# Products of w_out between the first scores of a delta rule, and the rule's level masks and spread rows on other engines

## What is computed

```
x += 0.5 * post1(FFN_a(pre1(x)))
h  = pre2(x);  u = h @ w_in          # columns for four mixers: pooling, RWKV-7, convolution, attention
x += post2(concat(A, B, C, D) @ w_out)
x += 0.5 * post3(FFN_b(pre3(x)))
```

```
s_kk = S @ kk
S    = S * w - outer(s_kk, kk * a) + outer(v, k)
y    = S @ r
```

## Time and profile before

| | |
|---|---|
| runs | 2569.2, 2569.83, 2566.56 us |
| the profiled execution's own time | 2568.88 us |
| its span, first to last instruction | 2567.1 us |
| mean granted clock of TensorE | 0.993 |
| PE busy | 2505.6 us, 98% |
| DVE busy | 1535.0 us, 60% |
| POOL busy | 1000.2 us, 39% |
| ACT busy | 945.5 us, 37% |

### The profile page before, as it was taken

One profiled execution on the slowest core, in us unless ns is written; L12 is line 12 of the kernel. 1 busy time (PEld: TensorE's weight loads), 2 busy tenths in 40 slices (PEclk: granted clock), 3 DMA queues, 4 the chain that ended last, 5 costly groups with the idle time before them and its releaser, 6 DMA issues.

```text
span 2567.1 us, 49724 instructions
## 1 busy us (share of the span) xinstructions
PE 2505.6 (98%) x20230; PEld 2444.3 (95%) x20230; DVE 1535.0 (60%) x2361; ACT 945.5 (37%) x1500; POOL 1000.2 (39%) x584
## 2 busy tenths in 40 slices
PE   8999999999899999999999999999998999999998
PEld 8999999999789999999999999998987889999998
DVE  6767721866774767771277767038567657777603
ACT  5444511422522444441244444133144244444412
POOL 4454532532112544543344544334312044545431
PEclk9999999999999999999999999999999999999999
DMA  4232222323102232222222232222230022222221
GB/s 118 85 88 82 82 72 61 97 58 94 45 3 76 58 91 82 82 85 73 74 66 82 82 90 76 76 79 70 68 98 17 11 67 83 82 82 82 83 77 64
DMA packets 356072, 188.64 MB, mean 73 GB/s; under 512 B 16330, under 2 KB 354086, under 8 KB 355912
## 3 DMA queue, kind: packets, MB, share of 16 engines
q1 hardware_dynamic: 355668, 186.25, 25.1%
q10 hardware_dynamic: 244, 0.08, 0.0%
HBM read 179.50 MB, written 6.80 MB: 73 GB/s over the span
## 4 chain that ended last, share of the span: by engine, by line
PE 88%; DVE 6%; DVEq 2%; ACT 2%; issue 1%; ACTq 0%; DMA 0%; SPq 0%
PE ps L1848 14%; PE ps L1850 13%; PE ps L1849 13%; PE ps L1971 12%; PE ps L1970 12%; PE ps L1969 12%; PE ps L1894 3%; PE ps L1837 1%; DVE xT L1197 1%; DVE ps L1193 1%; PE ps L2396 1%; PE ps L2414 1%; DVE h_split L1217 1%; PE ps L2410 1%; PE ps L2084 1%
## 5 line engine op out<-in xcount | busy, mean ns | idle before, releaser
L643 POOL TENSOR_TENSOR w_lo<-w_raw,w_hi 128x1024 fp32r<-128x1024 f32 (+1 forms) x186 | 444.9, 2396 | 949.6 <-ACT w_hi L724 948.6
L1848 PE MATMUL ps<-h_split,w_hi 128*128 128x384 f32 (+1 forms) x1536 | 485.0, 316 | 2.7 <-DVEq L1304 2.7
L1850 PE MATMUL ps<-h_split,w_lo 128*128 128x384 f32 (+1 forms) x1536 | 476.9, 310 | 0.0
L1849 PE MATMUL ps<-hidden_lo,w_hi 128*128 128x384 f32 (+1 forms) x1408 | 433.1, 308 | 0.0
L724 ACT ACTIVATE w_hi<-w_raw 128x1024 fp32r<-128x1024 f32 (+1 forms) x186 | 188.9, 1020 | 507.8 <-DMA w_raw<-in_ffn_w_down 318.3
L1849 PE MATMUL ps<-h_split,w_hi 128*128 128x256 f32 (+1 forms) x1152 | 354.8, 308 | 0.0
L1848 PEld LDWEIGHTS ps<-h_split,w_hi 128*128 128x128 f32 x1536 | 288.6, 188 | 8.6 <-issue 7.7
L1850 PEld LDWEIGHTS ps<-h_split,w_lo 128*128 128x128 f32 x1536 | 291.1, 190 | 0.0
L662 POOL TENSOR_TENSOR w_lo<-w_raw,w_hi 128x512 fp32r<-128x512 f32 x144 | 186.2, 1293 | 254.9 <-DVEq L1332 254.9
L1970 PE MATMUL ps<-h_split,w_hi 128*128 128x320 f32 x864 | 266.4, 308 | 0.0
L1971 PE MATMUL ps<-h_split,w_lo 128*128 128x320 f32 x864 | 266.4, 308 | 0.0
(11 more groups left out here) (390 smaller groups left out, 5808.8 us busy)
## 6 DMA issues: line engine op xcount, KB each, us to landing
w_raw<-in_ffn_w_gate SPq DMA_DIRECT2D x88, 512.0 KB, 4.6
w_raw<-in_ffn_w_up SPq DMA_DIRECT2D x88, 512.0 KB, 3.8
w_raw<-in_ffn_w_down SPq DMA_DIRECT2D x64, 448.0 KB, 3.4
w_raw<-in_w_in SPq DMA_DIRECT2D x42, 512.0 KB, 4.1
w_raw<-in_ffn_w_down SPq DMA_DIRECT2D x32, 512.0 KB, 3.7
w_raw<-in_w_out SPq DMA_DIRECT2D x16, 512.0 KB, 3.8
token_rows<-in_x_prompt SPq DMA_DIRECT2D x4, 512.0 KB, 5.9
k_cache<-in_cache_sb_k SPq DMA_DIRECT2D x2, 1024.0 KB, 5.8
```

The source lines that it names most:

```text
L643: nc.gpsimd.tensor_tensor(WLO[s][:, 0:n], RAW[s][:, 0:n], WHI[s][:, 0:n].bitcast(F32), ALU.subtract).then_inc(sem(f"lo_ready{s}"), 1)
L1848: MM(out, hi, mov[0][:, cols], start=first, stop=False)
L1849: MM(out, hi, mov[1][:, cols], start=False, stop=False)
L1850: return MM(out, lo, mov[0][:, cols], start=False, stop=last)
```

## The change

1. Six chunks of w_out's tile 0 (`others`) are multiplied in the rule's first pair: two after each lane's scores, in place of the four dummies there, one ahead of the second level, one ahead of the second pair's scores. They are summed in set 0; ScalarE copies the sum to SBUF (OUT_PART), and TensorE's first chain step waits for that. After the rule, tile 1 takes the place that tile 0 had between the statistics and tile 2 that of tile 1; at "mixed" tile 0 gets its two rule rows in set 2, and VectorE adds OUT_PART when it takes the tile out. Tiles 3 and 4 follow as wholes. TensorE waits for tile 0's copy before it turns the states.
2. The masked blocks NT of the levels after the first are made by VectorE: the second level's ahead of the first level's updates, the others after the updates of the level two before.
3. The low parts of w_out's tiles 2 and 3 are made by VectorE, ahead of the rule and after its first pair. Tile 2 is rounded by ScalarE in the attention's iteration 5 (`PAST_AT + 1`).
4. The spread value rows NMK are made by ScalarE in four copies with a scale by row, in the second pair's levels two to five. GpSimd has no instruction left between the low part of w_out's tile 1 and that of tile 4.

The diff without the lists of step names, and with little of what surrounds it:

```diff
@@ -426,6 +426,7 @@
 INV_ROWS = XSF[:, 0:TT * G]
+OUT_PART = XS[:, 6, :]
@@ -489,6 +490,9 @@
     return 3 if m == 5 else m % 2
+def out_set(m):
+    return (2, 0, 1, 0, 1)[m]
@@ -691,23 +695,9 @@
         cross(l * 3 + 1)
-        for t in range(4, NW + 3):
+        for t in range(4, NW + 2):
             low(in_block(l) + t)
-        low(out_block(l) + 3)
-        for p, lanes in enumerate(PAIRS):
-            a, t = lanes[-1]
-            pool.wait_ge(sem("lt_ready"), l * TT + t + 1)
-            for v in range(1, LEVELS[p]):
-                if v >= 2:
-                    pool.wait_ge(sem(f"t1_in{a}"), lane_count(l, p, a, PROMPT_LEVELS, SAMPLE_LEVELS) + v - 1)
-                n = len(lanes)
-                nc.gpsimd.tensor_tensor(NT[:, v % 2, 0:n].rearrange("p a j n -> p (a j) n"), LA[:, 0:n].rearrange("p a j n -> p (a j) n"),
-                                        LEV[:, v + 1, :].unsqueeze(1).broadcast_to([P, n * NH, CH]), ALU.mult).then_inc(sem("blocks_ready"), 1)
-        pool.wait_ge(sem("values_out"), nth(l, "values_out"))
-        pool.wait_ge(sem("exps_ready"), (l + 1) * len(PAIRS))
-        nc.gpsimd.tensor_tensor(NMK, value_rows(PT).rearrange("p (h n) -> p h n", h=NH).unsqueeze(2).broadcast_to([P, NH, HSTR, HD]),
-                                ROWM.unsqueeze(1).unsqueeze(3).broadcast_to([P, NH, HSTR, HD]), ALU.mult).then_inc(sem("kappa_spread"), 1)
@@ -1040,6 +1030,8 @@
                 keep_sig(it + 2)
+            if it == PAST_AT + 1:
+                round_weights(out_block(l) + 2)
@@ -1056,13 +1048,15 @@
         act.drain().then_inc(sem("values_out"), 1)
-        round_weights(in_block(l) + NW + 2)
...
                 a, t = lanes[k]
+                if p == 1 and k == 0:
+                    act.wait_ge(sem("out_part_in"), nth(l, "out_part_in"))
+                    A(OUT_PART, pset(0), ACT.Copy).then_inc(sem("out_part_kept"), 1)
@@ -1089,6 +1083,13 @@
                 exps(p + 1)
+            elif v and p == 1:
+                kappa_spread(v - 1)
+        def kappa_spread(s):
+            if s == 0:
+                act.wait_ge(sem("masks_loaded"), (l + 1) * 16)
+            A(NMK[:, :, s, :], value_rows(PT).rearrange("p (h n) -> p h n", h=NH), ACT.Copy, scale=ROWM[:, s:s + 1]).then_inc(sem("kappa_spread"), 1)
@@ -1161,7 +1162,12 @@
                 dve.wait_ge(sem("wkv_stored"), (e // 3 + 1) * 5 * 16)
-            V.tensor_copy(Yb[:, m, :], pset(m % 2)).then_inc(sem("y_copied"), 1)
+            if e % 3 != 1:
+                V.tensor_copy(Yb[:, m, :], pset(m % 2)).then_inc(sem("y_copied"), 1)
+            elif m == 0:
+                V.tensor_tensor(Yb[:, m, :], pset(out_set(m)), OUT_PART, ALU.add).then_inc(sem("y_copied"), 1)
+            else:
+                V.tensor_copy(Yb[:, m, :], pset(out_set(m))).then_inc(sem("y_copied"), 1)
@@ -1698,6 +1704,16 @@
         dve.wait_ge(sem("masks_loaded"), (l + 1) * 16)
+        def out_low(m):
+            s, u = (out_block(l) + m) % NSLOT, (out_block(l) + m) // NSLOT
+            dve.wait_ge(sem(f"hi_ready{s}"), u + 1)
+            V.tensor_tensor(WLO[s][:], RAW[s][:], WHI[s][:].bitcast(F32), ALU.subtract).then_inc(sem(f"lo_ready{s}"), 1)
+        def level_blocks(p, v):
+            n = len(PAIRS[p])
+            V.tensor_tensor(NT[:, v % 2, 0:n].rearrange("p a j n -> p (a j) n"), LA[:, 0:n].rearrange("p a j n -> p (a j) n"),
+                            LEV[:, v + 1, :].unsqueeze(1).broadcast_to([P, n * NH, CH]), ALU.mult).then_inc(sem("blocks_ready"), 1)
@@ -1763,13 +1779,20 @@
+        out_low(2)
...
             v, update = divmod(k - len(PAIRS[p]), 2)
+            if v == 0 and not update:
+                level_blocks(p, 1)
+            if v >= 0 and update and v + 2 < LEVELS[p]:
+                level_blocks(p, v + 2)
...
                 operands(p + 1, (v - 1,))
+            if p == 0 and update and v + 1 == LEVELS[p]:
+                out_low(3)
@@ -2306,6 +2329,14 @@
+        b0 = out_block(l)
+        rule_rows, others = (2, 3), (0, 1, 4, 5, 6, 7)
+        def out_chunks(q, m, cs):
+            for c in cs:
+                end = products(q, (b0 + m) % NSLOT, c, chunk(c), c == others[0], m == 0 and c == others[-1])
+            return end
@@ -2337,7 +2368,9 @@
                 pe.wait_ge(sem("values_out"), nth(l, "values_out"))
-                busy(1, 4)
+                pe.wait_ge(sem("lo_split"), l + 1)
+                block_ready(b0)
+                out_chunks(0, 0, others[2 * a:2 * a + 2])
@@ -2374,6 +2407,8 @@
             if k < len(lanes):
+                if p == 1 and k == 0:
+                    out_chunks(0, 0, others[5:]).then_inc(sem("out_part_in"), 1)
@@ -2388,6 +2423,8 @@
                 else:
+                    if p == 0 and v == 1:
+                        out_chunks(0, 0, others[4:5])
@@ -2432,6 +2469,7 @@
                     pe.wait_ge(sem("attn_split"), nth(l, "attn_split"))
+                    pe.wait_ge(sem("out_part_kept"), nth(l, "out_part_kept"))
@@ -2467,13 +2505,6 @@
-        b0 = out_block(l)
-        rule_rows, others = (2, 3), (0, 1, 4, 5, 6, 7)
-        def out_chunks(m, cs):
-            for c in cs:
-                products(m, (b0 + m) % NSLOT, c, chunk(c), c == others[0], False)
@@ -2495,9 +2526,8 @@
-        pe.wait_ge(sem("lo_split"), l + 1)
-        block_ready(b0)
-        out_chunks(0, others[:3])
+        block_ready(b0 + 1)
+        out_chunks(0, 1, others[:3])
@@ -2511,7 +2541,7 @@
         pe.wait_ge(sem("spread_u"), l + 1)
-        pe.wait_ge(sem("kappa_spread"), l + 1)
+        pe.wait_ge(sem("kappa_spread"), (l + 1) * HSTR)
@@ -2523,28 +2553,29 @@
         end.then_inc(sem("inverse_spread"), 1)
-        out_chunks(0, others[3:4])
+        out_chunks(0, 1, others[3:4])
...
         end.then_inc(sem("sample_var_in"), 1)
-        out_chunks(0, others[4:])
+        out_chunks(0, 1, others[4:])
         pe.wait_ge(sem("sample_states"), nth(l, "sample_states"))
-        block_ready(b0 + 1)
-        out_chunks(1, others[:2])
+        block_ready(b0 + 2)
+        out_chunks(1, 2, others[:2])
...
         end.then_inc(sem("sample_inverse_spread"), 1)
-        out_chunks(1, others[2:])
+        out_chunks(1, 2, others[2:])
         pe.wait_ge(sem("mixed"), nth(l, "mixed"))
-        for m in (0, 1):
+        for m in (0, 1, 2):
             for c in rule_rows:
-                end = products(m, (b0 + m) % NSLOT, c, chunk(c), False, c == rule_rows[-1])
+                end = products(out_set(m), (b0 + m) % NSLOT, c, chunk(c), m == 0 and c == rule_rows[0], c == rule_rows[-1])
             used(end, b0 + m)
+        pe.wait_ge(sem("y_copied"), copies_before(l * 3 + 1) + 1)
@@ -2555,9 +2586,9 @@
         e = l * 3 + 1
-        for m in range(2, 5):
+        for m in (3, 4):
             pe.wait_ge(sem("y_copied"), copies_before(e) + m - 1)
-            whole(m % 2, b0 + m)
+            whole(out_set(m), b0 + m)
```

More of the change, by code:

```diff
@@ L163 @@
         "state_turned", "decay_in", "a_in", "gate_in", "kk_summed", "bonus_summed", "tails_turned", "v_turned", "pool_out", "k_turned",
-        "values_turned", "stateT_in", "state_rhs_in", "mean_in", "var_in", "sample_mean_in", "inverse_spread",
+        "values_turned", "out_part_in", "stateT_in", "state_rhs_in", "mean_in", "var_in", "sample_mean_in", "inverse_spread",
         "sample_var_in", "sample_inverse_spread", "sample_state_in", "prompt_state_in"),
@@ L167 @@
         "gates_ready", "decay_ready", "a_ready", "gate_ready", "kk_root", "pool_scaled", "k_out", "conv_hi", "pool_hi",
-        "attn_late_hi", "attn_sample_hi", "attn_hi", "values_out", "stateT_out", "state_rhs_out", "var_root", "sample_var_root",
+        "attn_late_hi", "attn_sample_hi", "attn_hi", "values_out", "out_part_kept", "stateT_out", "state_rhs_out", "var_root", "sample_var_root",
         "yr_hi", "sample_yr_hi", "sample_state_out", "prompt_state_out"),
```

## The result

The changed kernel took 2544.65 us (median of 6 runs, 2538.9 to 2547.3) against 2568.88 us of the kernel before (6 runs, 2566.6 to 2574.3) on the same chip: ratio 0.9898, 95% interval 0.9889 to 0.9908, that is 23.6 to 28.5 us less. Forecast were 19.8 us less. The direction and the terms that the sum priced came as forecast; the clock, which it left at nothing, did not, and the size is that of rival (a).

A forecast was written before the change was run, and what follows sets the result against it. TensorE was taken as full after the rule, the first pair as a hand-over chain stretched by VectorE waiting for GpSimd; 5.3 + 1.9 + 1.6 + 1.1 = 9.9 us a layer, 19.8 for two, gave 2549.4 us, range 2543.5 to 2559.

The forecast's parts named there:

- rival (a): TensorE's clock stays up: idleness ahead of both falls shrinks, half-clock stretches go, 4.2 us less, 2545.2 us; chance 0.15.
- first pair, scores to next scores: Rule's first pair: unstretched VectorE products net 2.2 us, less 0.2 for later masks and 0.1 for the sixth chunk: 1.9 us.
- second pair and the third's scores: Rule's second pair: two stretched VectorE products give 1.1 us each, less 0.6 for its first mask: 1.6 us a layer.
- third pair to the statistics: Rule's third pair: a stretched VectorE product returns to 0.29 us; TensorE's wait of 1.08 us goes, 1.1 us a layer.
- chunks, after the rule: After the rule TensorE issues 58 chunks of w_out instead of 64, at 0.89 us each: 5.3 us a layer.
- clock, both layers: Second layer's half-clock stretches, priced at some 4.2 us, were taken as unchanged because the same code shows both clocks.
- The weighed rule: Of a two-SBUF-input VectorE instruction beside a GpSimd one reading SBUF, the later is blocked until the first has finished.
- the 0.4 us of lateness: After the rule, an addition blocked for all 2.34 us makes tile 4 0.4 us late per layer: 2550.2 us.
- (b): The rule keeps its pace, VectorE spending what GpSimd's leaving gives back; only the products pay: 2558.6 us; chance 0.15.
- (c): Tile 4 or 5 comes late after the rule, by 1 to 2 us a layer: 2551.4 to 2553.4 us; chance 0.08.
- (d): Moved chunks, masks and low halves land on the path, 10.3 against a gross 11.4 us: 2567 us, no change; chance 0.05.
- (e): Slower: without the dummies TensorE's clock falls in the pairs of both layers, costing 55 us, 2604 us; chance 0.05.

The follow-up runs named there:

- engines-alone kernel: Kernel before with masks and two low halves on VectorE, spread rows on ScalarE, rounding moved; no chunks moved, dummies kept: 2553.96 us, ratio 0.9940.

## Why the prediction was right or wrong

The sum's terms, first layer, from the rows of before and after (and the engines-alone kernel's rows where they separate the parts):

| term, us a layer | forecast | measured |
|---|---|---|
| first pair, scores to next scores | 1.9 | 27.27 - 25.43 = 1.8 |
| second pair and the third's scores | 1.6 | 1.9 |
| third pair to the statistics | 1.1 | 1.3 |
| chunks, after the rule | 5.3 | 5.3 |
| all | 9.9 | 10.3 |
| clock, both layers | 0 | 4.3 to 5.3 in the rule |

- **The chunks after the rule** came to the tenth. Tile 4 was not late: the copy of tile 2 ends at 789.06 + 0.82 = 789.88 us, and TensorE goes from tile 3 to tile 4 at 790.15 without a wait, 0.3 us of margin as forecast. Tile 5's margin was smaller than the 2 us given: its low half, the first of the two from 793.27, ends at about 795.9 us, and TensorE wants it at 790.15 + 7.09 = 797.2: 1.3 us.
- **The weighed rule** (the Trainium skill, SBUF — State Buffer, "Who interferes with whom") held in its form. The addition of 2.50 us began at 786.44, 0.6 after GpSimd's low half of 785.86 to 788.26, and ended 0.7 us after it: blocked until the first had finished. The 0.4 us of lateness that I drew from it didn't come, since the addition began 0.6 us into GpSimd's work and not just behind its start.
- **First pair**: right in sum, by two misses. The engines alone bring 2.3 us (27.27 of the kernel before against 24.97), not 2.0: the levels' pace stayed 694.39 - 691.31 = 3.08 us, so the masks of levels two to four cost nothing where 0.2 were set. The fifth and sixth chunk, set at 0.1 together, cost 25.43 - 24.97 = 0.5. Once VectorE is early, the waits that should cover them are 0.82 and 0.65 us (the engines-alone kernel's rows), both shorter than a chunk's 0.89: the second level comes 0.2 us later than without chunks, the second pair's scores another 0.3.

```profile
692.51 1.25 PE L2407 MATMUL ps<-sb_qkv 64*64 64x64 f32 x32 [0.82 <-DVE sb_qkv L1745]
...
705.51 0.63 PE L1848 MATMUL ps<-consts,beta_kappa 128*128 128x128 f32 x4 [0.65 <-DVEq L1752]
```

- **Second and third pair**: 1.43 and 1.08 us of waiting went as forecast; the rest is 0.3 and 0.2 us better. The 0.3 lies between the second pair's third and fourth level, 4.41 us apart before and 4.13 after. In the kernel before VectorE has one more stretched product there, which the prediction did not count (1.49 us at 725.34); with the masks back on GpSimd it is 4.42 again. The 0.2 was not followed.
- **The step that failed** is the last paragraph of the sum, "One cost is left out of it, the clock ... I take no change, since the same code shows both": a term of 4.3 to 5.3 us was put at nothing, because only one of two layers fell. That was read as evidence against a link with the waits, and it wasn't. In the third pair the layers were not equal: the second, which fell in both profiles, waits 1.43 us and the first 1.08, and the prediction reads the first layer's row alone. In the first pair they were nearly equal, and there two layers were a sample of two from something that happens about every second time: the fall is in the second layer of one profile and in the first of the other. What the two layers of the kernel before lose together is what should have been set, 5.3 us in one profile (152.97 - 147.69), 4.3 in the other (149.12 + 150.60 - 2 x 147.69), with some 10 us of half clock in each. These two numbers are good to about 0.5 us, since a layer without half clock is not always 147.69 us long (the first pair without a fall took 27.27 us in one profile and 26.75 in the other). I had priced the two falls at 4.2 us, from 9 us of them. With 2 x 10.3 + 4.3 to 5.3 the sum is 25 to 26 us; measured were 25.7 between the profiled executions and 23.6 to 28.5 by the ratio.
- **Rivals.** (a) is what happened, in its reason too: 2545.2 us, at a chance of 0.15 that was too low; what stood ahead of the first pair's fall, the wait, was in the rows. (b), (c) and (d) did not come. (e) did not come either, and its premise found no support: the kernel without any dummy or chunk in the first pair kept its clock (0.9946 over 5 runs).

## What to carry to other kernels

Where a profile shows half-clock stretches, treat them as a rate and not as fixed places: look for the wait ahead of each, and if the change removes the wait, count the stretch times its frequency, at 0.4 to 0.5 us of time for each us of half clock where TensorE sets the pace (4.3 and 5.3 us for some 10 here), and nothing where it doesn't. Compare the waits of equal places before taking them as equal. A second profile of the unchanged kernel, or the mean clock of its runs, tells fixed from frequent. A GpSimd instruction beside a VectorE chain can cost the chain nearly its own length: the mask of 1.27 us made a product 1.13 us longer (1.54 in place of 0.41). A wait that is used as cover for moved work is to be measured after the change that shortens it.

## What the runs showed of the hardware that was not expected

- TensorE's half clock (1.2 in place of 2.4 GHz) follows waits of 1.3 to 3.2 us among the rule's small products often but not always, in 10 of the 23 places that the profiles here show: with GpSimd at work beside them (6 of 17) or at rest (4 of 6). It followed none of 29 waits of 1.05 to 1.08 us. Two waits of 2.07 us behind the scores brought none in four places, which may be chance.
- Dummy products alone took 1.5 to 6.2 us off the kernel before.
- The mean clock of a run explains much of what looked like noise: runs of the kernel before at 0.990 (3) and at 0.994 (10) lie 7 us apart on average, 0.3% of the time, more than what the forecast called measurable.
- A higher mean clock is not a shorter time: 0.9962 with the mixer's waits filled brought nothing; VectorE and ScalarE were busy for 4.8 and 4.7 of 5 us there.
